# A hybrid encoder layer on one core: spectra from sums over even and odd samples, frequency pairs by sum and difference, and the inverse transform behind the second gate

## The chip, the cores and the metric

The kernel runs on one core of a Trainium2 chip. The metric is the time of one launch on the device in microseconds (us). TensorE (PE in the profile, PEld its weight loads) multiplies, VectorE (DVE) and ScalarE (ACT) do the elementwise work, SyncE (SP) issues nearly all loads. GpSimd does nothing here.

## The reference

One encoder layer over 256 tokens of width 1024, in float32: two mixers side by side, merged by gates, then 32 experts. The part that is changed is the long convolution of the Hyena mixer:

```python
z = (v * x1).astype(jnp.float32)
L = z.shape[1]
Z = jnp.fft.rfft(z, n=2 * L, axis=1)
K = jnp.fft.rfft(kern, n=2 * L, axis=0)
y = jnp.fft.irfft(Z * K[None], n=2 * L, axis=1)[:, :L] + z * hy_bias.astype(jnp.float32)
return y.astype(dt) * x0
...
o = o * jax.nn.silu(r)                                   # the other mixer (GLA), normalised
merged = jax.nn.sigmoid(g_gla) * (o_gla @ w_branch_gla) + jax.nn.sigmoid(g_hy) * (o_hy @ w_branch_hy)
h = h + merged @ w_out
h = h + moe_ffn(rms_norm(h, norm2_w), router_w, ...)     # top 4 of 32 experts
```

## The kernel before

Five programs, one per engine, walk the same list of stages (`schedule()`, `STAGES`) and do their share of each in that order; an engine never overtakes within its own list. Between engines stand semaphores.

The front (up to some 366 us) consists of projections with float32 precision made from three passes. Weights come in chunks of 1 MB (`FRONT`, `CHUNKS`) through four ring slots, so a chunk is loaded once the chunk four places ahead of it is used up. A chunk holds two units. For each unit ScalarE casts a high part (`parts`, L1266) and VectorE subtracts it for the low part (L1531); four such buffers exist (`HI_BUFS`), so the parts of a unit follow the use of the unit four places ahead. Units named `tok` take TensorE twelve matmuls of 512 columns. r 0 and r 1 (the silu gate of GLA) are eight such units, gg, wg, gh, wh (the two gates and the two branch matrices, each with halves 0 and 1) four units per half.

The Hyena convolution is a transform by matrix: the tokens are two blocks of 128 (`a`), the 256 odd frequencies of a 512-point transform two blocks of 128 (`kc`), with real and imaginary part (`ri`), the channels two halves of 512. `zt` transposes the product z to token-major tiles. `spectrum` (L791) gives one tile of K (the filter's) or Z (the signal's) from two accumulating matmuls, one per block of tokens. ScalarE copies the K tiles to SBUF; VectorE multiplies Z tiles in PSUM by them (L1694 to L1700, complex product). `zbias` scales z by the bias. The inverse (`y`, L975) is eight tiles of four matmuls, from which VectorE makes the Hyena outputs (L1708, L1711).

`gated` (L1671) multiplies the normalised GLA output by silu(r); `oT` transposes it on TensorE (L729) and waits for all eight operations of `gated` (`onorm_ready`). Before the change the stages run: zt, K, zbias, Z, r 0, r 1, gated, y, oT, gg 0, wg 0, gh 0, wh 0, gg 1, wg 1, gh 1, wh 1, wo (with the transposes mT of the merged tokens), router, experts.

In SP's list the loads of the front stop before chunk gh 0 for a wait on the Hyena outputs, since expert chunks go into ring slots that held the spectra:

```python
first_late = CHUNK_OF["gh0", 0]
for c in range(FSLOTS, first_late):
    front(c)

sp.wait_ge(ohy_ready, DB)
...
for c in range(first_late, len(CHUNKS)):
    for n in early[:1]:
        moe(n)
    early = early[1:]
    front(c)
```

`early` holds eight expert chunks of 1 MB. The other loads of the experts each wait until TensorE has used up what their slot held (`chunks_used`).

Of the kernel before, what the change touches and what calls it, by code (L numbers as in the profile page):

```python
# [97 lines left out]
def shape_tables():  # L98
# [11 lines left out]
    t[:, T_NEGT:T_NEGT + TB] = -lin.reshape(TB, P).T  # L110
# [4 lines left out]
    fwd = np.concatenate([np.cos(ang), np.sin(ang)], 1)  # L115
    inv = fwd.T / SEQ
    dft = np.concatenate([fwd.reshape(TB, P, 2 * SEQ).transpose(1, 0, 2).reshape(P, -1),
                          inv.reshape(4, P, SEQ).transpose(1, 0, 2).reshape(P, -1)], 1).astype(np.float32)
# [3 lines left out]
    z = np.concatenate([lin[:, None], np.cos(a), -np.sin(a)], 1).T.astype(np.float32)  # L122
    return np.ascontiguousarray(t), np.ascontiguousarray(dft), np.ascontiguousarray(z)
# [57 lines left out]
def schedule():  # L181
# [25 lines left out]
    for half in range(2):  # L207
        for k in ("gg", "wg", "gh", "wh"):
            if (k, half) == ("wh", 1):
                st += [("mT", 0), ("mT", 1)]  # L210
            st += tok(k, half)
            if (k, half) == ("wg", 0):
                st += [("ohy_parts",), ("bias_parts",)]
# [38 lines left out]
def tiles_of(stage):  # L252
# [8 lines left out]
    if kind in ("decay", "softplus", "energy", "energy_rest", "onorm", "gated", "zbias", "parts", "ohy_parts", "bias_parts", "wo"):  # L261
        return []
    if kind == "scores":
        return [f"sc{at[0]}", f"ke{at[0]}"]
    if kind == "updates":
        return [f"U{at[0]}{k}" for k in range(4)]
    if kind == "Z":
        return [f"Z{at[0]}{at[1]}{ri}" for ri in range(2)]
# [15 lines left out]
def build(nc, ins, out):  # L284
    plan, bank_uses = psum_plan()
    with ExitStack() as ctx:
# [62 lines left out]
        dft = hyreg(12288, 1024).rearrange("p (a k) -> p a k", a=TB)  # L349
        idft = hyreg(13312, 1024).rearrange("p (a t) -> p a t", a=4)  # L350
# [18 lines left out]
        ytmp = sumreg.rearrange("p (q a n) -> p q a n", q=2, a=2)  # L369
# [119 lines left out]
        z_ready = sem("z_ready")  # L489
        x0_ready = sem("x0_ready")  # L490
# [53 lines left out]
        def bank(name):  # L544
            return banks[plan[name][0]]
# [71 lines left out]
        def _(sp):  # L617
# [52 lines left out]
            sp.dma_start(hyreg(12288, 2048), ins["dft_table"]).then_inc(dft_loaded, 16)  # L670
# [48 lines left out]
        def _(pe):  # L719
# [114 lines left out]
            for stage in STAGES:  # L834
# [115 lines left out]
                elif kind == "zt":  # L950
# [3 lines left out]
                                                 zT[:, 4 * half + k, a * P:(a + 1) * P], ident) for k in range(4)])  # L954
                elif kind == "K":
                    ri, kc, half = at
                    pe.wait_ge(dft_loaded, 16)
                    pe.wait_ge(sd_ready, 2 * TB)
                    spectrum(f"K{ri}{kc}{half}", ri, kc,
                             lambda a: sumh[:, a, half * 512:(half + 1) * 512] if ri == 0 else  # L960
                             hf[:, a, D + half * 512:D + (half + 1) * 512])
                elif kind == "Z":
                    kc, half = at
                    if stage == ("Z", 0, 0):
                        for hh in range(2):
                            for a in range(TB):
                                emptied(pe, f"zt{a}{hh}")
# [956 lines left out]
```

## Time and profile before

| | |
|---|---|
| median of 3 runs | 1302.2 us (1301.52 to 1303.13) |
| the profiled execution | 1301.57 us, its span 1299.7 us |
| TensorE busy | 1201.0 us, 92% of the span |
| VectorE busy | 398.8 us, 31% |
| ScalarE busy | 264.7 us, 20% |
| moved from HBM | 454.26 MB, 350 GB/s over the span |
| TensorE's granted clock | 0.99 of full, mean of the span |

Busy time is the share in which an engine works on something; in which stretch it is the limit can't be told from it, only from the stretches and the chain of waits.

### The profile page before, as it was taken

Reading aid. Unit: us, or ns where it says so; the run is one execution under the profiler, and the core shown is the slowest. Engines: PE = TensorE matmul, PEld = TensorE weight load, DVE = VectorE, ACT = ScalarE, POOL = GpSimd, SP = SyncE. Lnnn points to the kernel's source line nnn. Section 1 sums busy time; section 2 is a strip of 40 time slices with the busy share of each in tenths; the row PEclk is TensorE's granted clock in tenths of the full one; section 3 lists DMA queues with packets and bytes.
Section 4 is the critical chain, followed back from the end, with each engine's and each line's share of the span. In section 5 each row is a group of like instructions: output and inputs, shape, how many; then the busy total and the mean of one; then the engine's idle time right before and its main releaser. Section 6 shows DMA issues by size and latency. Waiting matters only on the chain.

```text
span 1299.7 us, 14020 instructions
## 1 busy us (share of the span) xinstructions
PE 1201.0 (92%) x5992; PEld 619.0 (48%) x5992; DVE 398.8 (31%) x683; ACT 264.7 (20%) x398; POOL 0.2 (0%) x4
## 2 busy tenths in 40 slices
PE   6999999999999999999999888998898898889985
PEld 5889966888853343343334333332432243243321
DVE  6588837655541111121111111111111112111111
ACT  5855443344420010010001001000100010010001
POOL 0000000000000000000000000000000000000000
PEclk9999999999999989999999999999999999999999
DMA  9353423596599999999999999999999999999994
GB/s 328 106 153 109 143 76 98 176 385 209 198 352 407 425 410 428 428 429 427 429 427 428 427 428 428 429 427 427 429 427 428 427 427 428 427 428 429 428 426 202
DMA packets 66075, 456.25 MB, mean 351 GB/s; under 512 B 6777, under 2 KB 23450, under 8 KB 38876
## 3 DMA queue, kind: packets, MB, share of 16 engines
q1 hardware_dynamic: 64292, 454.52, 85.8%
q8 instruction: 49, 0.80, 0.3%
q10 hardware_dynamic: 1720, 0.82, 0.2%
q14 instruction: 14, 0.11, 0.0%
HBM read 454.26 MB, written 1.05 MB: 350 GB/s over the span
## 4 chain that ended last, share of the span: by engine, by line
PE 61%; DMA 29%; DVE 5%; ACT 3%; issue 2%; SPq 0%; ACTq 0%; DVEq 0%
DMA ring<-in_w_gate_up 28%; PE bank L1051 20%; PE bank L1067 12%; PE total L764 7%; PE bank L764 3%; PE total L752 3%; PE bank L752 3%; PE bank L807 3%; PE bank L1032 1%; PE bank L831 1%; PE bank L1058 1%; PE total L795 1%; PE bank L795 1%; ACT xn_area L1427 1%; PE total L1078 1%
## 5 line engine op out<-in xcount | busy, mean ns | idle before, releaser
L1051 PE MATMUL bank<-ring,hy_area 128*64 128x512 f32 x2048 | 456.9, 596 | 39.4 <-DMA ring<-in_w_gate_up 39.1
L1051 PEld LDWEIGHTS bank<-ring,hy_area 128*64 128x64 f32 x2048 | 140.1, 137 | 328.8 <-issue 248.1
L1067 PE MATMUL bank<-ring,xn_area 128*64 128x512 f32 x1024 | 231.5, 605 | 21.6 <-ACT xn_area L1427 21.6
L1830 DVE TENSOR_SCALAR qk_area<-bank 128x512 f32<-128x512 f32 x32 | 22.1, 692 | 426.4 <-PE bank L1051 426.4
L1067 PEld LDWEIGHTS bank<-ring,xn_area 128*64 128x64 f32 x1024 | 71.8, 139 | 159.9 <-issue 131.6
L1423 ACT ACTIVATE qk_area<-qk_area 128x512 f32<-128x512 f32 x32 | 20.2, 631 | 496.4 <-DVE qk_area L1830 496.4
L1843 DVE SCALAR_TENSOR_TENSOR xn_area_r<-bank,tmp_area,xn_area_r 128x512 fp32r<-128x512 f32 x32 | 24.0, 751 | 308.3 <-ACT xn_area_r L1432 308.3
L1531 DVE TENSOR_TENSOR front_r<-ring,slot_r 128x1024 fp32r<-128x1024 f32 x66 | 80.6, 1223 | 51.5 <-ACT slot_r L1266 51.5
L1266 ACT CAST slot_r<-ring 128x1024 fp32r<-128x1024 f32 x66 | 69.1, 1047 | 68.2 <-PE total L764 44.2
L1432 ACT ACTIVATE xn_area_r<-bank,tmp_area 128x512 fp32r<-128x512 f32 x32 | 22.0, 687 | 234.7 <-PE bank L1067 234.7
L831 PE MATMUL bank<-tmp_area_r 128*128 128x512 f32 x128 | 39.6, 432 | 7.0 <-DVE qk_area L1831 5.3
L764 PE MATMUL total<-front_r,slot_r 128*128 128x512 f32 x112 | 43.8, 391 | 0.0
L1078 PE MATMUL total<-xn_area_r 64*128 64x512 f32 x256 | 38.3, 417 | 1.7 <-DVE xn_area_r L1843 1.7
L1427 ACT COPY xn_area<-bank 128x512 f32<-128x512 f32 x32 | 18.8, 586 | 87.7 <-PE bank L1058 87.7
L1078 PEld LDWEIGHTS total<-xn_area_r 64*128 64x128 f32 x256 | 21.6, 184 | 30.5 <-issue 25.2
L764 PE MATMUL total<-slot_r 128*128 128x512 f32 x88 | 34.3, 390 | 0.0
L831 PEld LDWEIGHTS bank<-tmp_area_r 128*128 128x128 f32 x128 | 22.0, 192 | 21.6 <-DVE qk_area L1831 16.2
L1058 PE MATMUL bank<-tab,qk_area 128*128 128x128 f32 x128 | 23.4, 309 | 8.7 <-DVE qk_area L1838 8.7
L764 PE MATMUL total<-slot_r,xn_area_r 128*128 128x512 f32 x76 | 30.5, 402 | 1.0 <-DVE xn_area_r L1547 1.0
L1531 DVE TENSOR_TENSOR front_r<-ring,w_hi_late 128x1024 fp32r<-128x1024 f32 x22 | 26.9, 1223 | 14.6 <-ACT w_hi_late L1266 14.5
L764 PE MATMUL bank<-front_r,slot_r 128*128 128x512 f32 x80 | 31.3, 392 | 0.0
L1058 PEld LDWEIGHTS bank<-tab,qk_area 128*128 128x128 f32 x128 | 19.4, 209 | 18.9 <-issue 18.2
(323 smaller groups left out, 1208.0 us busy)
## 6 DMA issues: line engine op xcount, KB each, us to landing
ring<-in_w_gate_up SPq DMA_DIRECT2D x116, 2048.0 KB, 30.6
ring<-in_w_down SPq DMA_DIRECT2D x58, 2048.0 KB, 34.5
ring<-in_w_in SPq DMA_DIRECT2D x31, 1024.0 KB, 5.7
ring<-in_w_gate_up SPq DMA_DIRECT2D x24, 1024.0 KB, 8.9
ring<-in_w_down SPq DMA_DIRECT2D x12, 1024.0 KB, 8.1
ring<-in_w_branch_gla SPq DMA_DIRECT2D x4, 1024.0 KB, 7.2
ring<-in_w_branch_hy SPq DMA_DIRECT2D x4, 1024.0 KB, 5.9
ring<-in_w_out SPq DMA_DIRECT2D x4, 1024.0 KB, 5.2
```

What stands on the lines that cost most here:

```text
L752: last = pe.matmul(t[:, 0:SEQ], w[:, d, :], act[:, d, :], start=(m == 0 and d == 0), stop=(m == 2 and d == DB - 1))
L764: last = pe.matmul(bank(f"{kind}{half}{a}")[:, :], act[:, d, a * P:(a + 1) * P], w[:, i, :], start=(u == 0 and i == 0 and m == 0), stop=(u ...
L795: last = pe.matmul(t[:, :], dft[:, a, ri * SEQ + kc * P:ri * SEQ + (kc + 1) * P], src(a), start=(a == 0), stop=(a == TB - 1))
L807: last = pe.matmul(banks[bank_of][:, i * width:(i + 1) * width], src[:, a, d_cols(d)], moving, start=(m == 0 and a == 0), stop=(m == 1 and ...
L831: pe.matmul(banks[bk][:, :], b_pick[e % 2][:, bk * P:(bk + 1) * P], part, start=(m == 0), stop=(m == 1))
L1051: last = pe.matmul(banks[bk][half * CAP:(half + 1) * CAP, :], xeT[:, j, q, :], slot(where(j))[:, c:c + 512], start=False, stop=(j == GU_CH ...
L1058: last = pe.transpose(banks[3][:, c * P:(c + 1) * P], act[:, c:4 * P:4], ident)
L1067: last = pe.matmul(banks[2][half * CAP:(half + 1) * CAP, :], half_of(actT, f), slot(where(j))[:, c * D + half * 512:c * D + (half + 1) * 512],
L1078: last = pe.matmul(banks[4 + 2 * a + half], selT[r, q, a * P:(a + 1) * P], part[r, :], start=False, stop=True, skip_group_check=True)
L1266: nc.scalar.copy(unit_hi(j), unit_of(j)).then_inc(w_hi_ready, 1)
L1427: nc.scalar.copy(actT.rearrange("p c s -> p (c s)"), banks[3][:, :]).then_inc(actT_ready, 1)
L1531: nc.vector.tensor_tensor(unit_of(j, as_r["front"]), unit_of(j), unit_hi(j).bitcast(F32), ALU.subtract).then_inc(w_parts_ready, 1)
```

## The change

The block of tokens `a` is now a sample parity: token 2p + a in partition p. A frequency k and its mirror 255 - k have the same sum over even samples and the opposite one over odd samples (with the roles of sum and difference exchanged in the imaginary part). So one matmul per parity and part gives a tile `even` and a tile `odd`; their sum is the spectrum at the lower 128 frequencies, their difference that at the upper ones. ScalarE copies the odd tile to SBUF, VectorE adds and subtracts (`combine`). Z is then in SBUF (`zparts`), and its product with K (`Zmul`) is six operations of 2 x 512 columns per half of the channels. The stages now run: zt, K, Z, r 0 (first two units), Zmul 0, r 0 (rest), zbias, r 1 (first two units), Zmul 1, r 1 (rest), gated, oT, gg 0, wg 0, gg 1, y, wg 1, gh 0, wh 0, gh 1, wh 1, and the chunks of weights are loaded in this order. The tables, the filter features and the transposes are permuted to match.

```diff
-         ("gg0", "w_in", GG0), ("wg0", "w_branch_gla", 0), ("gh0", "w_in", GH0), ("wh0", "w_branch_hy", 0),
-         ("gg1", "w_in", GG0 + HALF), ("wg1", "w_branch_gla", HALF), ("gh1", "w_in", GH0 + HALF),
-         ("wh1", "w_branch_hy", HALF)]
+         ("gg0", "w_in", GG0), ("wg0", "w_branch_gla", 0), ("gg1", "w_in", GG0 + HALF), ("wg1", "w_branch_gla", HALF),
+         ("gh0", "w_in", GH0), ("wh0", "w_branch_hy", 0), ("gh1", "w_in", GH0 + HALF), ("wh1", "w_branch_hy", HALF)]
...
-    st += [("K", ri, kc, half) for ri in range(2) for kc in range(2) for half in range(2)] + [("zbias",)]
-    st += [("Z", kc, half) for kc in range(2) for half in range(2)]
-    st += tok("r", 0) + tok("r", 1) + [("gated",)]
-    st += [("y", b) for b in range(DB)] + [("oT", n) for n in range(4)]
...
+    st += [("K", ri, half) for ri in range(2) for half in range(2)] + [("Z", half) for half in range(2)]
+    r0, r1 = tok("r", 0), tok("r", 1)
+    st += r0[:2] + [("Zmul", 0)] + r0[2:] + [("zbias",)] + r1[:2] + [("Zmul", 1)] + r1[2:] + [("gated",)]
+    st += [("oT", n) for n in range(4)] + tok("gg", 0) + tok("wg", 0) + tok("gg", 1)
+    st += [("y", b) for b in range(DB)] + tok("wg", 1) + [("ohy_parts",)] + tok("gh", 0) + [("bias_parts",)] + tok("wh", 0)
+    st += tok("gh", 1) + [("mT", 0), ("mT", 1)] + tok("wh", 1)
...
-            sp.dma_start(hyreg(12288, 2048), ins["dft_table"]).then_inc(dft_loaded, 16)
+            sp.dma_start(hyreg(12288, 1536), ins["dft_table"]).then_inc(dft_loaded, 16)
...
-            def spectrum(name, ri, kc, src):
-
-                t = begin(name)
-                for a in range(TB):
-                    last = pe.matmul(t[:, :], dft[:, a, ri * SEQ + kc * P:ri * SEQ + (kc + 1) * P], src(a),
-                                     start=(a == 0), stop=(a == TB - 1))
-                last.then_inc(fill(name), 1)
+            def spectrum(name, ri, a, src):
+
+                pe.matmul(begin(name)[:, :], dft[:, a, ri * P:(ri + 1) * P], src, start=True, stop=True).then_inc(fill(name), 1)
...
-                                                 zT[:, 4 * half + k, a * P:(a + 1) * P], ident) for k in range(4)])
+                                                 zT[:, 4 * half + k, a::TB], ident) for k in range(4)])
...
-                    pe.wait_ge(Y_ready, 4)
+                    pe.wait_ge(Y_ready, b // 4 + 1)
...
+            def combine(even, odd, ri, plus, minus):
+
+                filled(dve, even)
+                emptied(dve, odd)
+                nc.vector.tensor_tensor(plus, bank(even)[:, :], minus, ALU.add)
+                if ri == 0:
+                    last = nc.vector.tensor_tensor(minus, bank(even)[:, :], minus, ALU.subtract)
+                else:
+                    last = nc.vector.tensor_tensor(minus, minus, bank(even)[:, :], ALU.subtract)
+                last.then_inc(empty(even), 1)
...
+                elif kind == "Zmul":
+                    half, = at
                     cs = slice(half * 512, (half + 1) * 512)
...
+                    emptied(dve, "K110")
+                    emptied(dve, f"Z{half}10")
+                    zr, zi = zparts[half][:, 0], zparts[half][:, 1]
+                    kr, ki = Kf[:, 0, :, cs], Kf[:, 1, :, cs]
+                    nc.vector.tensor_tensor(Yf[:, 0, :, cs], zr, kr, ALU.mult)
+                    link(nc.vector.tensor_tensor(Yf[:, 1, :, cs], zr, ki, ALU.mult))
+                    nc.vector.tensor_tensor(zr, zi, ki, ALU.mult)
+                    nc.vector.tensor_tensor(zi, zi, kr, ALU.mult).then_inc(z_multiplied, 1)
+                    dve.wait_ge(z_multiplied, half + 1)
+                    nc.vector.tensor_tensor(Yf[:, 0, :, cs], Yf[:, 0, :, cs], zr, ALU.subtract)
+                    nc.vector.tensor_tensor(Yf[:, 1, :, cs], Yf[:, 1, :, cs], zi, ALU.add).then_inc(Y_ready, 1)
```

The instructions move as the following listings of the two programs show (in order, without times). First VectorE from the end of the spectra to `gated` in the kernel before. L1531 is the low part of a unit, L1731 the product of r with its sigmoid, L1671 `gated`.

```order
L1699 TENSOR_TENSOR ring<-ring 128x512
L1700 TENSOR_TENSOR ring<-ring 128x512
L1531 TENSOR_TENSOR front_r<-ring,slot_r 128x1024 x3
L1731 TENSOR_TENSOR gla_area<-total,tmp_area 128x512 x2
L1531 TENSOR_TENSOR front_r<-ring,w_hi_late 128x1024
L1531 TENSOR_TENSOR front_r<-ring,slot_r 128x1024 x3
L1731 TENSOR_TENSOR gla_area<-total,tmp_area 128x512 x2
L1531 TENSOR_TENSOR front_r<-ring,w_hi_late 128x1024
L1671 SCALAR_TENSOR_TENSOR v_area<-v_area,small,gla_area 128x256 x8
L1708 SCALAR_TENSOR_TENSOR ring<-bank,small,ring 128x256
L1711 TENSOR_TENSOR hy_area<-ring,hy_area 128x256
```

In the changed kernel the same place begins with the parts of two units and the six operations of Zmul 0. L1542 is the low part of a unit, L1746 the product of r, L1690 `zbias`.

```order
L1542 TENSOR_TENSOR front_r<-ring,slot_r 128x1024 x2
L1708 TENSOR_TENSOR ring<-gla_area,ring 128x2x512
L1709 TENSOR_TENSOR ring<-gla_area,ring 128x2x512
L1710 TENSOR_TENSOR gla_area<-gla_area,ring 128x1024
L1711 TENSOR_TENSOR gla_area<-gla_area,ring 128x1024
L1713 TENSOR_TENSOR ring<-ring,gla_area 128x2x512
L1714 TENSOR_TENSOR ring<-ring,gla_area 128x2x512
L1542 TENSOR_TENSOR front_r<-ring,slot_r 128x1024
L1746 TENSOR_TENSOR gla_area<-total,tmp_area 128x512 x2
L1542 TENSOR_TENSOR front_r<-ring,w_hi_late 128x1024
L1690 TENSOR_SCALAR ring<-ring,colw 128x256 x8
```

The list goes on with two parts and the first five operations of Zmul 1; from its sixth on it reads as follows, with L1682 as `gated` and L1558 as the first work behind `oT`.

```order
L1714 TENSOR_TENSOR ring<-ring 128x2x512
L1542 TENSOR_TENSOR front_r<-ring,slot_r 128x1024
L1746 TENSOR_TENSOR gla_area<-total,tmp_area 128x512 x2
L1542 TENSOR_TENSOR front_r<-ring,w_hi_late 128x1024
L1682 SCALAR_TENSOR_TENSOR v_area<-v_area,small,gla_area 128x256 x8
L1558 SCALAR_TENSOR_TENSOR gla_area_r<-bank,colw,v_area_r 128x256 x8
```

The two blocks of six now stand between the parts, and `gated` comes behind both of them; before, nothing of the spectra stood behind the first part of these.

SP's queue around the wait for the Hyena outputs, before: the wait stands ahead of the first row with `in_b_gate_up`, L654 is an expert chunk, L635 a front chunk.

```order
L635 DMA ring<-in_w_branch_gla 128x4x512 x2
L677 DMA tmp_area<-in_b_gate_up 128x512
L654 DMA ring<-in_w_gate_up 128x2048
L635 DMA ring<-in_w_in 128x4x512
L654 DMA ring<-in_w_gate_up 128x2048
L635 DMA ring<-in_w_in 128x4x512
```

And in the changed kernel:

```order
L635 DMA ring<-in_w_in 128x4x512 x2
L635 DMA ring<-in_w_branch_gla 128x4x512 x2
L677 DMA tmp_area<-in_b_gate_up 128x512
L654 DMA ring<-in_w_gate_up 128x2048
L635 DMA ring<-in_w_in 128x4x512
L654 DMA ring<-in_w_gate_up 128x2048
L635 DMA ring<-in_w_in 128x4x512
```

The chunks of gg 1 and wg 1 have moved ahead of the wait; the chunks behind it begin with gh 0 as before. Between the inverse and gh 0 TensorE had eight units (gg 0, wg 0); now it has four (wg 1).

## Rows read from the trace of the kernel before

**Rows 1.** first line of the page

```profile
span 1299.7 us, 14020 instructions
```

**Rows 2.** stretches: us, busy (instructions) of PE, PEld, DVE, ACT, POOL, granted clock, DMA share, GB/s

```profile
178.00:206.00 28.00, 28.00 (x72) 12.70 (x70) 12.48 (x28) 7.13 (x15) 0.00 (x0) 1.00 0.07 26
...
228.00:242.00 14.00, 14.00 (x67) 12.29 (x66) 11.36 (x26) 1.53 (x2) 0.00 (x0) 1.00 0.22 75
266.00:288.00 22.00, 22.00 (x98) 18.04 (x97) 11.91 (x11) 11.66 (x13) 0.00 (x0) 1.00 1.02 381
...
700.00:1250.00 550.00, 492.70 (x2315) 186.76 (x2311) 87.21 (x159) 42.07 (x72) 0.00 (x0) 0.99 1.01 428
```

**Rows 3.** chain of waits, 170 to 400 us: start us, us, what

```profile
178.70 6.87 PE total L795 x16
...
206.16 21.98 PE total L764 x96
228.14 6.91 PE bank L975 x32
...
241.95 1.75 PE bank L729 x16
...
367.80 1.94 PE bank L1051 x8
```

**Rows 4.** order of time, VectorE, 168 to 262 us: start us, busy us, line, operation

```profile
178.84 2.19 DVE L1679 TENSOR_SCALAR ring<-ring,colw 128x256 f32<-128x256 f32 x8
196.00 0.69 DVE L1694 TENSOR_TENSOR ring<-total,ring 128x512 f32<-128x512 f32 x1 [14.97 <-PE total L795]
196.61 0.68 DVE L1695 TENSOR_TENSOR ring<-total,ring 128x512 f32<-128x512 f32 x1
...
197.81 0.68 DVE L1697 TENSOR_TENSOR ring<-total,ring 128x512 f32<-128x512 f32 x1
198.52 0.69 DVE L1699 TENSOR_TENSOR ring<-ring 128x512 f32<-128x512 f32 x1
...
212.80 1.23 DVE L1531 TENSOR_TENSOR front_r<-ring,slot_r 128x1024 fp32r<-128x1024 f32 x1 [0.68 <-ACT slot_r L1266]
...
230.94 3.25 DVE L1671 SCALAR_TENSOR_TENSOR v_area<-v_area,small,gla_area 128x256 f32<-128x256 f32 x8
234.11 0.48 DVE L1708 SCALAR_TENSOR_TENSOR ring<-bank,small,ring 128x256 f32<-128x256 f32 x1
```

**Rows 5.** order of time, VectorE, 66 to 84 us

```profile
78.59 1.22 DVE L1597 TENSOR_TENSOR gla_area<-gla_area 128x1024 f32<-128x1024 f32 x1
79.72 1.22 DVE L1597 TENSOR_TENSOR ring<-ring 128x1024 f32<-128x1024 f32 x1
```

**Rows 6.** chain of waits, 78 to 104 us

```profile
85.56 7.45 PE bank L752 x48
...
97.18 5.75 PE total L752 x48
```

**Rows 7.** order of time, TensorE, 78 to 100 us (in brackets: idle before)

```profile
85.56 2.01 PE L752 MATMUL bank<-xn_area_r,slot_r 128*128 128x256 f32 x8 [1.97 <-DVE tmp_area L1639]
```

**Rows 8.** stretches, columns as in the second group

```profile
86.00:88.00 2.00, 2.00 (x11) 2.00 (x10) 1.97 (x4) 0.00 (x0) 0.00 (x0) 0.50 0.57 200
```

**Rows 9.** order of time, SP's queue, 0 to 480 us: issues

```profile
243.35 0.43 SPq L654 DMA_DIRECT2D ring<-in_w_gate_up  x1
...
276.71 0.38 SPq L635 DMA_DIRECT2D ring<-in_w_in  x1
```

**Rows 10.** order of time, ScalarE, 262 to 290 us

```profile
286.80 1.05 ACT L1266 CAST slot_r<-ring 128x1024 fp32r<-128x1024 f32 x1 [3.49 <-DMA ring<-in_w_in]
```

**Rows 11.** the line that loads front chunks (L635)

```profile
DMA to landing us min/median/max: 5.0/5.7/12.2
```

**Rows 12.** DMA issues, 240 to 300 us: queue, size of one, us to landing

```profile
tmp_area<-in_norm_f_w ACTq DMA_DIRECT2D x1, 512.0 KB, 17.3
...
tmp_area<-in_router_w ACTq DMA_DIRECT2D x1, 128.0 KB, 8.2
```

More of the change, by code:

```diff
@@ L114, in shape_tables @@
     ang = np.arange(SEQ)[:, None] * w[None, :]
[L115 to L118, printed above, removed]
+    fwd = np.concatenate([np.cos(ang[:, 0:P]), np.sin(ang[:, 0:P])], 1)
+    inv = (np.concatenate([np.cos(ang), np.sin(ang)], 1).T / SEQ).reshape(2, 2, P, SEQ)
+    inv[:, 1] = inv[:, 1, ::-1].copy()
+    dft = np.concatenate([fwd.reshape(P, 2 * SEQ), inv.reshape(4, P, SEQ).transpose(1, 0, 2).reshape(P, -1)], 1).astype(np.float32)
     omega = (np.float32(2.0 * np.pi) * np.arange(SEQ, dtype=np.float32) / np.float32(SEQ)).astype(np.float32)
@@ L122, in shape_tables @@
     z = np.concatenate([lin[:, None], np.cos(a), -np.sin(a)], 1).T.astype(np.float32)
+    z = np.concatenate([z[:, k::TB] for k in range(TB)], 1)
     return np.ascontiguousarray(t), np.ascontiguousarray(dft), np.ascontiguousarray(z)
@@ L260, in tiles_of @@
         return []
-    if kind in ("decay", "softplus", "energy", "energy_rest", "onorm", "gated", "zbias", "parts", "ohy_parts", "bias_parts", "wo"):
+    if kind in ("decay", "softplus", "energy", "energy_rest", "onorm", "gated", "zbias", "Zmul", "parts", "ohy_parts", "bias_parts", "wo"):
         return []
@@ L266, in tiles_of @@
         return [f"U{at[0]}{k}" for k in range(4)]
+    if kind == "K":
+        return [f"K{at[0]}{at[1]}{a}" for a in range(TB)]
     if kind == "Z":
-        return [f"Z{at[0]}{at[1]}{ri}" for ri in range(2)]
+        return [f"Z{at[0]}{ri}{a}" for ri in range(2) for a in range(TB)]
     return [kind + "".join(map(str, at))]
@@ L368, in build @@
         xbuf = ring[:, 4 * SLOT + 1024:5 * SLOT].rearrange("p (b t) -> p b t", b=4)
-        ytmp = sumreg.rearrange("p (q a n) -> p q a n", q=2, a=2)
+        zparts = [m.rearrange("p (r k n) -> p r k n", r=2, k=2) for m in (gla_area[:, :], sumreg)]
         zfeat = tmp_area[0:EMB, 0:SEQ]
@@ L489, in build @@
         z_ready = sem("z_ready")
+        z_multiplied = sem("z_multiplied")
         x0_ready = sem("x0_ready")
@@ L1333, in _ @@
                 elif kind == "K":
-                    ri, kc, half = at
-                    n = f"K{ri}{kc}{half}"
-                    copy_tile(n, Kf[:, ri, kc, half * 512:(half + 1) * 512], bank(n)[:, :])
+                    ri, half = at
+                    n = f"K{ri}{half}1"
+                    copy_tile(n, Kf[:, ri, 1, half * 512:(half + 1) * 512], bank(n)[:, :])
+                elif kind == "Z":
+                    half, = at
+                    for ri in range(2):
+                        n = f"Z{half}{ri}1"
+                        copy_tile(n, zparts[half][:, ri, 1, :], bank(n)[:, :])
                 elif kind == "zt":
@@ L1404, in _ @@
                         elif nm == "gg":
-                            emptied(sc, f"wh0{a}" if half else f"r1{a}")
+                            emptied(sc, f"wg0{a}" if half else f"r1{a}")
                             sigmoid_tile(n, a, empty(n))
                         elif nm == "gh":
-                            emptied(sc, f"wg{half}{a}")
+                            emptied(sc, f"wh0{a}" if half else f"wg1{a}")
                             sigmoid_tile(n, a, empty(n))
@@ new lines, in _ @@
+                elif kind == "K":
+                    ri, half = at
+                    even, odd = f"K{ri}{half}0", f"K{ri}{half}1"
+                    plus, minus = (Kf[:, ri, k, half * 512:(half + 1) * 512] for k in range(2))
+                    combine(even, odd, ri, plus, minus)
+                elif kind == "Z":
+                    half, = at
+                    for ri in range(2):
+                        combine(f"Z{half}{ri}0", f"Z{half}{ri}1", ri, zparts[half][:, ri, 0, :], zparts[half][:, ri, 1, :])
+                elif kind == "Zmul":
+                    half, = at
+                    cs = slice(half * 512, (half + 1) * 512)
+                    emptied(dve, "K110")
[9 more added lines that the diff above has]
+                    nc.vector.tensor_tensor(Yf[:, 1, :, cs], Yf[:, 1, :, cs], zi, ALU.add).then_inc(Y_ready, 1)
```

50 lines of the change are left out of this document (12 added, 38 removed).

## The prediction

> **What bounds the kernel now.** First the stretches, for who is busy where [rows 2]. In the spectra (178 to 206 us) and the inverse (228 to 242) TensorE is busy all of the time at the full clock while the DMA engines are nearly idle (share 0.07 and 0.22); from 266 to 288 TensorE is full and so are the DMA engines, at 381 GB/s; from 700 us on the DMA engines are full at 428 GB/s and TensorE has holes. So two bounds follow each other: TensorE up to the experts, the expert weights behind it. Then the chain of waits, for what links the pieces [rows 3]: spectra, r units, inverse, oT, gates follow one another on TensorE with no wait between. The expert stream can't start before that chain is through, because the expert chunks reuse ring slots which the queue frees by TensorE's progress. Its length is bytes over 428 GB/s. I therefore take a shift of TensorE's chain ahead of the experts one to one into the end. The profiled execution took 1301.57 us with a span of 1299.7 us [rows 1]; the median of the three runs is 0.6 us higher.
>
> **What is removed.** The spectra, four pieces of the chain like the first (6.87 us), from 178.70 us to the start of r at 206.16 us, are 32 matmuls of 512 columns: 27.5 us, 0.86 us each [rows 3]. The change issues 16. TensorE saves 13.7 us and would start r at 192.4 us. Each even/odd pair takes TensorE 1.72 us, ScalarE one copy, VectorE two operations that start 0.60 us apart [rows 4]: 1.2 us per pair, so VectorE keeps up here, and it ends the eighth pair near 194 us.
>
> **What is added, and where it lies.** The product of spectra was 24 operations of 512 columns on VectorE, most of it under the second half of the spectra. Now it is two blocks (Zmul) of six operations of 1024 columns, each block in VectorE's queue ahead of work that TensorE needs. Prices: 512 columns, starts 0.60 us apart, 0.71 us where a semaphore is waited for; a 1024 column operation from SBUF to SBUF, starts 1.13 us apart [rows 4, 5]. A block is 6 x 1.13 plus two waits of 0.11: 7.0 us.
>
> VectorE before Zmul 0 must do the parts of two r1 units. In the trace the second of these starts 6.64 us after r begins (212.80 against 206.16) [rows 3, 4] and waits for ScalarE, not for VectorE's queue. So it starts at 192.4 + 6.6 = 199.1, and Zmul 0 at 200.2. From there VectorE never waits; the queue in order of the listing is
>
> 7.0 (Zmul 0) + 1.1 (part) + 1.2 (two r products) + 1.1 (part) + 2.3 (zbias, 2.19 and its wait [rows 4]) + 2.3 (two parts) + 7.0 (Zmul 1) + 1.1 + 1.2 + 1.1 + 3.2 (gated, 230.94 to 234.11 [rows 4]) = 28.7 us,
>
> so gated ends at 228.9 us. The r units on TensorE take 21.98 us and end at 214.4. Their weights come just in time: the third r1 unit's part is done at 207.2 + 1.2 = 208.4, TensorE asks for it after six units of 2.75 us at 208.9. Behind r the next thing on TensorE is oT, which waits for all of gated, and in its queue stand gg 0 and everything else. Before, the inverse transform (228.14 to 241.95, 13.8 us [rows 3]) lay over gated and hid it; the change has moved that cover behind gg 1. TensorE idles from 214.4 to 229.0: 14.6 us. oT began at 241.95 with the inverse done; it now begins at 229.0 with 13.8 us of inverse owed: 242.8. **First term: +0.9 us**, the saved 13.7 us are gone in this wait.
>
> On these durations the Trainium skill (VectorE: DVE Perf Modes, The DRAIN you can't avoid) says that the next operation can't start before the pipe of the last one is empty, so that starts would stand a whole duration apart. The rows show 0.60 us between starts of operations that last 0.69 us, so the measurement decides; by the page the 28.7 us would be about 31 and the total some 2.4 us later.
>
> **The clock after the wait.** The one place ahead of the experts where TensorE, after steady work, stood still for about 2 us is at 83.6: restarted at 85.56, it was granted 0.50 of its clock (1.2 GHz) and 48 matmuls took 7.45 us, the same 48 later 5.75 us [rows 6 to 8]. That is 1.7 us for a wait of 2.0 us; a wait of 14.6 us should cost as much. No row shows a wait that long, so the bounds are 0 and, if the transposes of oT (1.75 us) also run at half speed beside it, 3.5 us. **Second term: +1.7 us.**
>
> **The weights behind the inverse.** SP waits for the last of the hyena outputs before it issues the bias, the first expert chunk and then chunk gh 0. It is a wait that stands ahead of all later loads. Before, it ended at 243.35, 1.4 us after the inverse, and gh 0 was 22 us away. Now the inverse ends with only wg 1 (11.0 us) ahead of gh 0. Call the inverse's end 0. First expert chunk issued at 1.4; a 1 MB load alone lands in 5.0 us [rows 9, 11]; chunk gh 0 lies behind it, 1.05 MB at 381 GB/s, 2.75 us: 9.2. Cast and part 2.3 us: ready at 11.5, wanted at 11.0. Stall 0.5 us. After that each chunk comes with an expert chunk, 2.1 MB at 381 GB/s, 5.5 us, exactly what TensorE needs for two units. Before, a chunk issued at 276.71 was waited for by ScalarE until 286.80, ten microseconds [rows 9, 10], and TensorE lost nothing since its lead was larger. Now that lead is gone, and the router's and norm's loads (128 and 512 KB from ScalarE's queue, the latter 17.3 us in flight [rows 12]) fall in the middle: 1.7 us at that rate, of which I count 1.5. **Third term: +2.0 us**; bounds 0 (the stream catches up, as 428 GB/s would allow) and 4 (the inefficient small loads cost double).
>
> The Trainium skill (DMA: Bandwidth & Descriptors, Specifications) names a limit of about 358 GB/s of HBM per core; by it a pair would take 5.9 us, and eight pairs would add some 3 us more. The trace has 381 to 428 GB/s on one core, above that limit, and I don't use it.
>
> **Edits at nothing.** The transform table is 0.25 MB shorter: it was loaded 160 us before its use. Strided transposes (zt): the same four tiles; TensorE's price of a step of two isn't in the trace, below 1.8 us if it doubled and 0 if it is free; I take 0, since the combination of halves is what follows. The swap of gg 1/wg 1 with gh 0/wh 0 keeps the number of units. zbias is counted above. The inverse's own products on VectorE stay hidden under its matmuls, as now. ScalarE's cast of the hyena outputs (and VectorE's part of it) now stands behind the gh 0 casts and so behind their loads; it is wanted at wh 0, 11 us after gh 0 begins, and stays hidden unless that chunk is several microseconds late.
>
> **Sum.** 1301.6 + 0.9 + 1.7 + 2.0 = 1306.2 us for the profiled execution, so 1306.5 us beside the median.
>
> **Rivals.**
> - *VectorE keeps up, faster.* If the queue from 200.2 were done by 214.4, the whole 13.7 us would be kept, less the third term: 1302.2 - 11.7 = 1290.5 us. For it the 28.7 us of work would have to be 14.2. To come out faster by over 2.6 us it must be under 21.5 us. Single steps are measured, and even the twelve operations of 1024 columns at half their price (as zbias, one-source, runs 256 columns in 0.27 us) give back only 6.4 us. The Trainium skill (VectorE: DVE Perf Modes, The perf-mode tier table) gives that double rate in fp32 to one-source operations and not to tensor_tensor. Chance 0.07.
> - *No change.* The first term alone, with the clock quickly back and the loads hidden: 1303.1 us; up to 1304.8 with one of them. For it speaks that both other terms are small against their uncertainty. Chance 0.20.
> - *Much slower.* The stalls in gh and wh are long enough to bring the half clock once more for each (1.7 us), and the small loads cost double: 1306.5 + 2 + 1.7 = 1310 us or more. Against it: the waits are under 1 us each. Chance 0.10.
> - *Forecast.* 1304.8 to 1309.5 us. Chance 0.60. The remaining 0.03 is for faster by a part of the queue, around 1298 us.
>
> **How the numbers follow.** This kernel's three runs lie about 0.1% apart, so a difference of 0.2% (2.6 us) can be told. Faster 0.10, same 0.20, slower 0.70. For 8 in 10 the range takes in the forecast, the no-change case and the near part of much slower: 1302.6 to 1310.0 us.
>
> **What will show it.** (1) Spectra: 16 matmuls, r starting near 192.4. (2) Zmul operations starting 1.13 us apart, VectorE without a gap from 200 to 229. (3) TensorE waiting some 14 us at oT for VectorE's gated. If that wait is under 7 us, the forecast is wrong. (4) granted clock 0.5 behind it. (5) a wait for DMA on the way to gh 0, and later ones of a microsecond at most. (6) the experts' first matmul, at 367.80 before [rows 3], near 372.4. If TensorE's chain is late by that but the end isn't, the one-to-one step is wrong.

## The result and the profile after

The changed kernel takes 1310.85 us (median of 8 runs, 1306.93 to 1312.68) against 1302.25 us before (8 runs, 1301.52 to 1305.97): 1.0058 times as long, 95% interval [1.0042, 1.0073]. It is slower, by 0.6%. The median lies 0.85 us above the top of the range (1310.0), and in the rival *much slower* (1310 us or more) rather than in the forecast (1304.8 to 1309.5); the ratio times the 1302.2 us that the prediction stood against is 1309.8, just inside the range. The profiled execution took 1308.84 us, 7.3 us more than the profiled one of before and inside the forecast.

First the chain of waits of the changed kernel, 170 to 400 us (start us, us, what). L793 are the spectra, L764 the units, L729 the transposes, L970 the inverse.

```profile
176.76 2.01 PE bank L729 x16
178.76 3.44 PE total L793 x8
...
192.50 5.50 PE total L764 x24
...
225.85 3.26 DVE v_area L1682 x8
229.16 3.68 PE bank L729 x16
232.83 22.14 PE total L764 x96
...
265.97 3.45 PE bank L970 x16
...
279.78 11.01 PE bank L764 x48
290.79 2.15 issue
292.94 23.86 PE total L764 x96
...
374.93 1.94 PE bank L1046 x8
```

Against [rows 3]: the spectra take 13.7 us, not 27.5, and r starts at 192.50 instead of 206.16. But the chain then leaves TensorE: from 200 us on it runs through VectorE up to `gated`, and oT (L729) starts at 229.16. The same 16 transposes that took 1.75 us now take 3.68. A piece called "issue" (time in which the engine waited for nothing that the profile shows) stands ahead of gh 0, and the 96 matmuls behind it take 23.86 us where their like take 21.99. The experts' first matmul stands at 374.93 against 367.80, 7.13 us later.

TensorE's waits of the changed kernel (us in total, times, longest) name the two new ones; the first is for `gated`.

```profile
PE bank L729 <- DVE v_area L1682: 14.6, 1, 14.6
...
PE total L764 <- issue: 2.2, 1, 2.2
```

VectorE of the changed kernel in order of time, 200 to 232 us:

```profile
200.30 1.22 DVE L1708 TENSOR_TENSOR ring<-gla_area,ring 128x1024 f32<-128x1024 f32 x1
201.43 1.22 DVE L1709 TENSOR_TENSOR ring<-gla_area,ring 128x1024 f32<-128x1024 f32 x1
...
210.82 2.19 DVE L1690 TENSOR_SCALAR ring<-ring,colw 128x256 f32<-128x256 f32 x8
213.05 2.36 DVE L1542 TENSOR_TENSOR front_r<-ring,slot_r 128x1024 fp32r<-128x1024 f32 x2
215.32 1.22 DVE L1708 TENSOR_TENSOR ring<-ring 128x1024 f32<-128x1024 f32 x1
...
225.85 3.25 DVE L1682 SCALAR_TENSOR_TENSOR v_area<-v_area,small,gla_area 128x256 f32<-128x256 f32 x8
```

From the row at 200.30 on no row ends in a bracket, and a bracket would name idle time: VectorE is occupied from Zmul 0 (L1708, 200.30) to the end of `gated` (229.1), 28.8 us without a gap. That answers to the queue that was summed from [rows 4, 5].

The stretches of the changed kernel (columns as in [rows 2]):

```profile
214.00:229.00 15.00, 0.51 (x3) 0.08 (x1) 14.93 (x20) 1.53 (x2) 0.00 (x0) 0.68 0.22 70
229.00:232.00 3.00, 2.84 (x14) 2.85 (x15) 0.10 (x1) 0.00 (x0) 0.00 (x0) 0.50 0.00 0
289.00:312.00 23.00, 20.85 (x84) 16.65 (x83) 13.45 (x12) 12.05 (x13) 0.00 (x0) 0.93 1.03 405
...
700.00:1250.00 550.00, 495.35 (x2324) 190.06 (x2325) 86.71 (x160) 42.24 (x72) 0.00 (x0) 0.98 1.01 428
```

The first row is the swap of bounds in one line: TensorE 0.51 us busy, VectorE 14.93 of 15. The second is the clock behind it, 0.50 (1.2 GHz). The last shows the experts as before, 428 GB/s: from the experts' first matmul to the end of the span it is 932.1 us (1307.0 - 374.93), before 931.9.

Last the loads behind the inverse: SP's queue of the changed kernel in order of time, ScalarE's first cast of gh 0, and the time from issue to landing (last number, us) of the first expert chunk and of the first chunk of gh 0. They answer to [rows 9 to 12].

```profile
280.79 0.34 SPq L677 DMA_DIRECT2D tmp_area<-in_b_gate_up  x1
281.18 0.43 SPq L654 DMA_DIRECT2D ring<-in_w_gate_up  x1
281.65 0.43 SPq L635 DMA_DIRECT2D ring<-in_w_in  x1
282.13 0.50 SPq L654 DMA_DIRECT2D ring<-in_w_gate_up  x1
```

```profile
290.54 1.99 ACT L1261 CAST slot_r<-ring 128x1024 fp32r<-128x1024 f32 x2 [22.95 <-DMA ring<-in_w_in]
```

```profile
ring<-in_w_gate_up SPq DMA_DIRECT2D x1, 1024.0 KB, 6.7
ring<-in_w_in SPq DMA_DIRECT2D x1, 1024.0 KB, 8.9
```

The first chunk of gh 0 is issued at 281.65 and in use at 290.54, as soon as it has landed: 8.9 us. TensorE asked for its parts at 290.79 and got them at 292.94.

### The profile page after: what moved, and what is told of

The parts are those of the page before. It is cut to its first block, busy times and chain, and to the rows that moved or that the text cites. A ratio compares the mean times of both kernels' runs of the same rounds, so it can differ in the third digit from the quotient of the medians.

```text
span 1307.0 us, 13963 instructions
## 1 busy us (share of the span) xinstructions
PE 1193.2 (91%) x5960; PEld 616.9 (47%) x5960; DVE 407.3 (31%) x687; ACT 263.8 (20%) x398; POOL 0.2 (0%) x4
## 4 chain that ended last, share of the span: by engine, by line
PE 59%; DMA 29%; DVE 7%; ACT 3%; issue 2%; SPq 0%; DVEq 0%; ACTq 0%
DMA ring<-in_w_gate_up 28%; PE bank L1046 20%; PE bank L1062 12%; PE total L764 6%; PE bank L764 3%; PE total L752 3%; PE bank L752 3%; PE bank L803 3%; PE bank L1027 1%; PE bank L827 1%; PE bank L1053 1%; DVE front_r L1542 1%; ACT xn_area L1427 1%; PE total L1073 1%; DMA ring<-in_w_in 1%
## 5 line engine op out<-in xcount | busy, mean ns | idle before, releaser
L1062 PE MATMUL bank<-ring,xn_area 128*64 128x512 f32 x1024 | 234.2, 611 | 21.6 <-ACT xn_area L1427 21.6
L1542 DVE TENSOR_TENSOR front_r<-ring,slot_r 128x1024 fp32r<-128x1024 f32 x66 | 80.2, 1222 | 58.2 <-ACT slot_r L1261 58.1
L764 PE MATMUL total<-front_r,slot_r 128*128 128x512 f32 x128 | 50.8, 396 | 0.0
L764 PE MATMUL total<-slot_r 128*128 128x512 f32 x100 | 39.6, 396 | 0.0
L764 PE MATMUL total<-slot_r,xn_area_r 128*128 128x512 f32 x76 | 31.5, 415 | 3.1 <-issue 2.2
L1542 DVE TENSOR_TENSOR front_r<-ring,w_hi_late 128x1024 fp32r<-128x1024 f32 x22 | 26.9, 1222 | 12.3 <-ACT w_hi_late L1261 12.3
L764 PEld LDWEIGHTS total<-front_r,slot_r 128*128 128x128 f32 x128 | 24.6, 192 | 5.3 <-issue 0.2
## 6 DMA issues: line engine op xcount, KB each, us to landing
ring<-in_w_branch_hy SPq DMA_DIRECT2D x4, 1024.0 KB, 13.8
```

Of the source, the lines that this page charges most:

```text
L764: last = pe.matmul(bank(f"{kind}{half}{a}")[:, :], act[:, d, a * P:(a + 1) * P], w[:, i, :], start=(u == 0 and i == 0 and m == 0), stop=(u ...
L1062: last = pe.matmul(banks[2][half * CAP:(half + 1) * CAP, :], half_of(actT, f), slot(where(j))[:, c * D + half * 512:c * D + (half + 1) * 512],
L1542: nc.vector.tensor_tensor(unit_of(j, as_r["front"]), unit_of(j), unit_hi(j).bitcast(F32), ALU.subtract).then_inc(w_parts_ready, 1)
```

## The experiments

The theory on trial is that of the prediction: VectorE's queue up to `gated` bounds TensorE, the clock falls in the wait, and chunk gh 0 is late. The rivals: the order of the stages costs the time whatever VectorE does; the even and odd spectra cost it; the loads alone do. Each kernel below is timed beside the kernel before on the same chip.

**Zmul 1 behind `gated`.** It takes six operations of 1024 columns out of the queue ahead of `gated`.

```diff
-    st += r0[:2] + [("Zmul", 0)] + r0[2:] + [("zbias",)] + r1[:2] + [("Zmul", 1)] + r1[2:] + [("gated",)]
+    st += r0[:2] + [("Zmul", 0)] + r0[2:] + [("zbias",)] + r1 + [("gated",), ("Zmul", 1)]
```

> The changed kernel with Zmul 1 moved behind gated in the list of stages, nothing else. Theory (VectorE's queue from Zmul 0 to gated is the wait at oT): the queue is 7.0 us shorter, oT is released near 222.1 us instead of 229.1, TensorE's wait there falls from 14.6 to 7.6 us, the half clock behind it stays, and the whole is 7 us shorter than the changed kernel: about 1304 us beside its median of 1311, ratio to the kernel before 1.001. Rival (oT is held by something other than that queue, such as r's last product or the banks): the wait stays near 14.6 us and the time near 1311 us, ratio 1.006.

Measured: 1301.77 us (11 runs) beside 1302.53 (19 runs), ratio 0.9994 [0.9983, 1.0005]. The median is 2.2 us below the 1304 us expected. TensorE's wait at oT and the chain of waits:

```profile
PE bank L729 <- DVE v_area L1682: 7.6, 1, 7.6
```

```profile
221.89 3.68 PE bank L729 x16
...
283.82 2.18 issue
286.00 22.20 PE total L764 x96
```

The wait fell by 7.0 us, the price of one block, and oT starts 7.3 us sooner. So VectorE's queue is what TensorE waits for there, and one block is enough to bring back the time of before. Half the wait costs the same half clock (3.68 us again). The rest of the gain, to 8.5 us at the experts' first matmul (366.40), is that the 2.18 us at gh 0 brought no half clock this time: 22.20 us instead of 23.86. Some 0.3 us of it was lost again in gg 0 and wg 0 (22.44 us instead of 22.14).

**The chunks of gh 0 ahead of SP's wait.** Both chunks of gh 0 are issued before SP waits for the Hyena outputs.

```diff
-            first_late = CHUNK_OF["gh0", 0]
+            first_late = CHUNK_OF["wh0", 0]
```

> The changed kernel, but SP issues the two chunks of gh 0 before its wait for the Hyena outputs. Theory (the wait ahead of these loads costs a stall and a half clock): the stall of 2.15 us ahead of gh 0 and the 1.9 us of half clock behind it go, 4 us less than the changed kernel: 1307 us, ratio 1.003. Rival (the DMA engines are too slow for front and expert chunks together): the stall appears at wh 0 or gh 1 instead, with its half clock, and the time stays at 1311, ratio 1.006.

Measured: 1306.38 us (9 runs) beside the same 1302.53, ratio 1.0029 [1.0019, 1.0038]. The chain of waits has no piece ahead of gh 0 any more, and its units are at their full rate:

```profile
278.81 11.01 PE bank L764 x48
289.81 21.99 PE total L764 x96
```

From the end of wg 1 to the first matmul of the experts it is 80.1 us (289.82 to 369.92), in the changed kernel 84.1 (290.79 to 374.93): in the traces the late chunk costs 4.0 us, 2.15 of wait and 1.87 of half clock. The medians bear out the direction and not the size: this one is 4.5 us below the changed kernel's first median and 1.7 below the one of the second series (1308.12, below). The wait at oT stays at 14.7 us; the two are independent of each other.

**The order alone.** The spectra of before (four accumulating pairs and a VectorE product under them) in the changed order: oT, gg 0, wg 0, gg 1, y, wg 1, gh 0, with the chunks and ScalarE's waits to match.

```diff
-    st += [("y", b) for b in range(DB)] + [("oT", n) for n in range(4)]
...
+    st += [("oT", n) for n in range(4)] + tok("gg", 0) + tok("wg", 0) + tok("gg", 1)
+    st += [("y", b) for b in range(DB)] + tok("wg", 1) + [("ohy_parts",)] + tok("gh", 0) + [("bias_parts",)] + tok("wh", 0)
```

> The kernel before with only the order changed: the inverse behind gg 1, gg 1 and wg 1 ahead of gh 0, the loads in that order; spectra and products as before. Theory: r ends at 228.1, gated at 234.1, so TensorE waits 6.0 us at oT, which the inverse covered; half clock 2.0 us; gh 0 late and half clock 4.0 us: 12 us slower than before, about 1314 us, ratio 1.009. Rival (the order is harmless and the spectra's form costs the time): within 3 us of the kernel before, ratio 1.000 to 1.002.

Measured: 1312.54 us (5 runs) beside 1302.53, ratio 1.0079 [1.0064, 1.0093]. Chain of waits:

```profile
230.78 3.26 DVE v_area L1665 x8
...
234.08 3.30 PE bank L723 x16
...
295.17 0.79 issue
```

Here `gated` (L1665) ends where it ended before, and oT (L723) stands directly behind it: TensorE waits 6.1 us, with r ended at 228.0. Before, those 6.1 us lay under the inverse. With the inverse owed, oT comes 5.9 us later than before (234.08 + 13.81 against 241.95), its transposes take 1.55 us more, and most of the rest are two waits of 0.8 us for parts of gh 0 and behind. So the order by itself costs 10 us; 12 were expected, since the wait at gh 0 was taken over from the changed kernel. SP issues the same loads here in the same rhythm (first expert chunk at 285.56, chunk gh 0 at 286.03), but they land sooner, measured from issue as above:

```profile
ring<-in_w_gate_up SPq DMA_DIRECT2D x1, 1024.0 KB, 5.3
ring<-in_w_in SPq DMA_DIRECT2D x1, 1024.0 KB, 7.5
```

**The spectra alone.** The changed kernel with the order of before: y ahead of oT, then gg 0, wg 0, gh 0, wh 0 and the second halves. All of the even and odd work and both Zmul blocks stay where the change put them.

```diff
-    st += [("oT", n) for n in range(4)] + tok("gg", 0) + tok("wg", 0) + tok("gg", 1)
-    st += [("y", b) for b in range(DB)] + tok("wg", 1) + [("ohy_parts",)] + tok("gh", 0) + [("bias_parts",)] + tok("wh", 0)
...
+    st += [("y", b) for b in range(DB)] + [("oT", n) for n in range(4)]
```

> The changed kernel with the order undone: the inverse directly behind r and gated, gates and loads in the order of before; spectra from even and odd samples, sums and differences and the Zmul blocks stay. Theory: TensorE does the inverse's first half from 214.4, waits about 1 us for Zmul 1 (222.4), ends the inverse near 229.3; oT follows gated and the inverse's first products on VectorE, done near 232.6; gg 0 starts near 233.1 instead of 243.7, and gh 0 has its lead again: 10.6 us less than before, about 1291.7 us, ratio 0.992. Rival (the Zmul blocks on VectorE cost what the halved spectra save): ratio 0.999 to 1.003.

Measured: 1290.86 us (5 runs) beside 1302.53, ratio 0.9909 [0.9896, 0.9923]. TensorE in order of time (L976 is the inverse, L735 oT; in brackets the idle time before):

```profile
222.24 7.17 PE L976 MATMUL total<-ring 128*128 128x256 f32 x32 [1.12 <-DVE ring L1720]
230.22 0.63 PE L735 MATMUL bank<-tab,v_area 128*128 128x128 f32 x4 [0.23 <-DVE ring L1728]
```

The inverse stands over `gated` again, and what is left of the wait is 1.1 us for Zmul 1 in the middle of the inverse and under 1 us around oT. gg 0 starts at 232.78, the first matmul of the experts at 357.12, 10.7 us earlier than before. This is 20.0 us faster than the changed kernel's first median and 17.3 us faster than its second, from the order alone. The rival in which VectorE keeps up was worked out to 1290.5 us. That the measured time is so near is in part chance: its sum has the third term (2.0 us), which this kernel doesn't pay, and of the 13.7 us saved it loses 3.0 up to the experts, 2.0 of them in these waits.

**The changed kernel once more, and the wait filled.** The first of these is the kernel unaltered, to have its time beside the next ones. The second puts 16 matmuls of 512 columns, whose results are overwritten, ahead of oT's wait. TensorE then has something to do in it; nothing on VectorE moves.

```diff
+                    if stage == ("oT", 0):
+                        t = begin("oT0")
+                        for _ in range(16):
+                            pe.matmul(t[:, :], ident, tab[:, 0:512], start=True, stop=True)
                     pe.wait_ge(onorm_ready, 8)
```

> The changed kernel once more, unaltered, for a second trace. Its eight runs fall into two groups (1307 to 1309 and 1310 to 1313 us). In the traces so far the stretch from the experts' first matmul to the end took 931.9 to 932.1 us, but 936.7 in one run in which TensorE was at 0.91 of its clock in the first 80 us of it. If the spread lies there, a run near 1311 us has about 935 us in this stretch and the front up to 375 us as before; if it lies ahead of it (the terms of the prediction vary), the experts begin near 378 us.

> The changed kernel, with 16 more matmuls (identity times a table, 13.7 us, into the bank that oT overwrites) on TensorE ahead of its wait at oT; they add nothing to the result. Theory of the clock: the wait of TensorE shrinks to 0.9 us, oT takes 1.75 instead of 3.68 us, gg 0 starts 2.1 us earlier: 1308.8 us. Rival (oT is slow for another reason, its operands or its banks): oT stays at 3.7 us.

Measured: unaltered 1308.12 us (10 runs), ratio 1.0045 [1.003, 1.006] to 1302.6 (21 runs); filled 1309.55 us (6 runs), ratio 1.0045 [1.0028, 1.0063]. Stretches of the filled one:

```profile
214.00:228.00 14.00, 13.31 (x32) 5.54 (x30) 13.93 (x19) 1.20 (x2) 0.00 (x0) 1.00 0.22 75
228.00:231.00 3.00, 2.79 (x21) 2.62 (x22) 0.15 (x1) 0.79 (x3) 0.00 (x0) 1.00 0.00 0
...
390.00:397.00 7.00, 6.31 (x20) 2.37 (x20) 1.87 (x4) 0.59 (x1) 0.00 (x0) 0.56 0.77 324
```

Chain of waits:

```profile
228.21 1.97 PE bank L729 x16
...
287.98 1.31 issue
289.30 22.24 PE total L764 x96
```

With TensorE busy up to 0.9 us before `gated` ends, oT runs at the full clock and takes 1.97 us instead of 3.68: the idling is what took the clock, and the term is 1.7 us in oT and some 0.1 in the 96 matmuls behind it (22.00 us, 22.14 and 22.05 unfilled). At the experts' first matmul (370.39) the kernel is 4.0 us ahead of the unaltered one (374.43). Only 1.8 us of that are this term: the wait at gh 0 was also shorter (1.31 us, 2.26 in the unaltered kernel), with 0.25 us of half clock behind it and not 1.83, and another wait of 0.5 us came ahead of wh 1. The time at the end doesn't show the gain: 1308.8 us were expected, from the first median of 1310.85, and beside the second the filled kernel isn't faster at all. From there to the end of the span it takes 937.2 us, not 931.8. The third row above is where it begins: 20 us into the experts TensorE is at 0.56 of its clock, the DMA share falls to 0.77, and in the first 50 us of the experts 375 GB/s are moved where the changed kernel moves 388 and the kernel before 393. I had not foreseen that, and come back to it below.

**zbias ahead of the spectra, in the spectra alone.** The eight operations of `zbias` go in front of K, where VectorE has time.

```diff
-    st += [("K", ri, half) for ri in range(2) for half in range(2)] + [("Z", half) for half in range(2)]
+    st += [("zbias",)] + [("K", ri, half) for ri in range(2) for half in range(2)] + [("Z", half) for half in range(2)]
...
-    st += r0[:2] + [("Zmul", 0)] + r0[2:] + [("zbias",)] + r1[:2] + [("Zmul", 1)] + r1[2:] + [("gated",)]
+    st += r0[:2] + [("Zmul", 0)] + r0[2:] + r1[:2] + [("Zmul", 1)] + r1[2:] + [("gated",)]
```

> The spectra alone (order of before), with zbias put back ahead of the spectra, where VectorE stands idle for 2.6 us. Theory of the queue: Zmul 1 is done at 220.1, before TensorE asks for it (221.3), gated ends near 226.8, gg 0 starts near 230.9 instead of 232.8: 1289.0 us, 1.9 us less than without, ratio 0.9895. Rival (what is left there is TensorE's own work): 1290.9, ratio 0.991.

Measured: 1292.24 us (6 runs, 1288.87 to 1293.88) beside 1302.6, ratio 0.9916 [0.9897, 0.9936]. Its profiled execution took 1288.87 us (1289.0 expected), gg 0 started at 230.98, 1.8 us ahead of 232.78, and the wait for Zmul 1 was gone, which is what moving 2.2 us of VectorE out of the queue should give. The median doesn't confirm a gain: the six times lie in two groups, 1288.9 to 1290.9 and 1293.6 to 1293.9. Between this kernel and the spectra alone the runs don't decide.

**The changed order, mended.** Zmul 1 behind `gated`, zbias ahead of K, chunks of gh 0 ahead of SP's wait: all three edits above, in the changed kernel.

> The changed order with all three remedies: Zmul 1 behind gated, zbias ahead of the spectra, the two chunks of gh 0 ahead of SP's wait. The queue up to gated is 28.7 - 7.0 - 2.3 = 19.4 us, the wait at oT falls to 5.3 us, the half clock behind it stays, nothing waits at gh 0: 14.6 - 5.3 + 4.0 = 13.3 us less than the changed kernel, about 1297 us, ratio 0.996. Rival (the terms hide one another): not under 1300 us.

Measured: 1296.47 us (6 runs) beside 1302.6, ratio 0.9948 [0.9931, 0.9965]. Chain of waits:

```profile
216.85 3.26 DVE v_area L1682 x8
220.15 3.67 PE bank L729 x16
223.83 22.40 PE total L764 x96
...
282.04 21.99 PE total L764 x96
```

About 1297 us were expected. The change can be made to pay with its own order, but 5.6 us (medians) less than the spectra alone, and 4.2 less than those with `zbias` early, which were timed in the same series. Of the wait at oT 6.1 us remain (5.3 expected), the same as with the order alone: it is the length of the last products of r, a part and `gated` behind the end of r, which no place for Zmul shortens, and it costs the half clock in oT (3.67 us) once more. That part belongs to a unit behind oT; `gated` ahead of it in VectorE's list wasn't tried.

## Why the prediction was right, and where it wasn't

The table has every profiled kernel at the three places that count, in us: start of oT, first matmul of the experts, and from there to the end of the span.

| kernel | oT | experts | to the end | its run | median |
|---|---|---|---|---|---|
| before | 241.95 | 367.80 | 931.9 | 1301.57 | 1302.25 |
| changed | 229.16 | 374.93 | 932.1 | 1308.84 | 1310.85 |
| changed again | 228.68 | 374.43 | 931.8 | 1308.05 | 1308.12 |
| Zmul 1 behind gated | 221.89 | 366.40 | 936.7 | 1304.87 | 1301.77 |
| gh 0 chunks ahead | 228.72 | 369.92 | 932.0 | 1303.79 | 1306.38 |
| order alone | 234.08 | 377.71 | 933.0 | 1312.54 | 1312.54 |
| spectra alone | y first | 357.12 | 931.9 | 1290.86 | 1290.86 |
| zbias early | y first | 355.28 | 931.8 | 1288.87 | 1292.24 |
| order mended | 220.15 | 362.18 | 932.5 | 1296.53 | 1296.47 |
| wait filled | 228.21 | 370.39 | 937.2 | 1309.54 | 1309.55 |

*What is removed*: right. 13.7 us of matmuls are gone, r starts at 192.50 (192.4 said).

*VectorE's queue*: right in its parts and its sum. Zmul operations start 1.13 to 1.26 us apart; the queue took 28.8 us (28.7 said; its parts as they are printed add up to 28.6) and TensorE waited 14.6 us (14.6 said). The **first term** was +0.9 and measured +1.0: 229.16 + 13.81 of inverse owed, less 241.95. That the wait is VectorE's is shown by taking one block out of the queue (7.0 us less wait), and that the inverse was the cover by giving it back (spectra alone). The Trainium skill (VectorE: DVE Perf Modes, The DRAIN you can't avoid) has the next operation start when the pipe of the one before is empty, but adds that one which isn't held back starts earlier. The prediction left the second half out. The trace agrees with it: 1.22 us operations start 1.13 us apart (200.30, 201.43), and 28.8 us stand against the estimate of 31 by the first half alone. One example in the rival *VectorE keeps up* was misread as well: 256 columns in 0.27 us is 1.1 us for 1024, the price of the operations in Zmul and not half of it.

*The clock after the wait*: right. The **second term** was +1.7 and measured +2.1: 1.93 in oT, 0.15 in gg 0. A wait of 14.6 us costs about what one of 2.0 us did in [rows 6] (1.7 us), as assumed. The filled wait shows that idling is the cause. That any wait of about 2 us does this isn't shown (see the last section).

*The weights behind the inverse*: the place and the mechanism were right, the size was not. This **third term** was mis-sized: +2.0 said, +4.0 measured, just at the bound of 4. It was made of 0.5 us of stall and 1.5 us for the router's and norm's loads. The runs showed the other way round. The stall was 2.15 us: with the inverse ended at 279.78, chunk gh 0 was in use 10.8 us later and not 9.2. The step behind that is the landing of the expert chunk ahead of it, 6.7 us where the 5.0 of a lone load was taken; chunk gh 0 followed it by 2.7 us, as said (2.75). The expert chunk took 6.7 to 6.8 us in three traces (changed, again, Zmul 1 behind `gated`), but 5.3 in the order alone and 5.6 in the filled kernel, behind the same bias and with the same chunks issued behind it; the stall was 0.79 and 1.31 us there. So neither the bias nor the four chunks issued within 1.5 us (281.18 to 282.68) explain the 6.7 us by themselves; why it differs stays open. And the stall brought 1.87 us of half clock, which was put into the rival *much slower*, on the reason that waits under 1 us bring none. The 1.5 us for the small loads never appeared: from the start of gg 0 to the experts' first matmul it was 124.1 us before (243.70 to 367.80); after it is 142.1 us, and less the inverse (13.81), the stall (2.15) and the two half clocks (1.87 and 0.15) that is 124.1 again. The chunks ahead of SP's wait gave this term back in the trace.

The Trainium skill (DMA: Bandwidth & Descriptors, Specifications) has about 358 GB/s of HBM as the limit for a core; the changed kernel's trace has 405 GB/s in 289 to 312 us and 428 in the experts on its one core, so the measurement decides against it as a limit here, and no stall past gh 0 came.

*One to one to the end*: right for the profiled executions, 932.1 against 931.9 us. 1.0 + 2.1 + 4.0 = 7.1 us is the whole of 374.93 - 367.80. It is not a law: the column "to the end" has two entries that are 5 us longer, and one that is 1.1 us longer.

*The sum*: the prediction says that the median was 0.6 us above the profiled execution, which makes 1306.8 us beside the median and not 1306.5; nothing hangs on it.

*Edits at nothing*: the strided transposes of z cost 0.2 us (2.01 for 16 against 1.80 before), bound 1.8; the others nothing that shows.

*The median*: 1310.85, 2.0 us above its own profiled execution, and 1308.12 when run again. The times of this kernel spread over nearly 6 us: 1306.9 to 1312.7 in the first series and 1306.6 to 1312.2 in the second, with a gap in the middle each time (1308.8 to 1310.3, 1309.3 to 1311.3); which side holds the median moves it. The kernel before spreads as much in the experiments' series, without such a gap (1300.6 to 1306.1, and one of 1308.2). Both traces of the changed kernel were from the lower side, so what its longer executions do wasn't seen. So the terms are tested on the profiled execution, 1306.2 said and 1308.84 measured, and not on whether the median falls inside the range.

Where did the gain go, then? The spectra alone are worth 11.7 us. The order alone costs 10.0. Together they should come out near 1301, and the unaltered kernel is 7 to 10 us above that (1308.12, 1310.85). The rest is the two meeting, in the traces 6.4 us up to the start of gg 0 and 1.6 at gh 0, where the order alone lost 2.4 us and the changed kernel 4.0. For the first: the spectra's work moved into VectorE's queue between r and `gated`, and the order took away the 13.8 us of TensorE's work that would have hidden it. Either alone can be afforded.

## What to carry to other kernels

Work taken off the busy engine and put on an idle one belongs behind the last thing that the busy engine will ask the idle one for, or under work that covers it, as in the spectra alone; the idle engine's average (31% here) says nothing about its queue in that stretch. Before a stage is moved, add up what it covered at its old place, on every engine and queue; here the inverse covered 6.1 us of the last step of the gate even before anything was added. Try the parts of a combined change one by one: half of this one is 0.9% faster, the other half 0.8% slower.

## What the runs showed of the hardware

**The same short wait has different prices.** At gh 0 TensorE waited 2.15 us in the changed kernel and 2.26 us when it was run again, and the next 96 matmuls took 23.86 and 23.82 us (the granted clock was 0.86 in 293 to 295 us and 0.50 in 295 to 297, so it fell after the restart, not in the wait). With Zmul 1 moved the wait was 2.18 us and the matmuls took 22.20, at a clock of 1.00 in 286 to 292. A 1.3 us wait in the filled kernel cost 0.25 us. The kernel before has such a pair too: the wait of 1.97 us of [rows 7] was followed by 0.50, one of 1.76 us that ended at 25.55 by a clock of 1.00 in 26 to 28. What decides between them isn't shown. At oT every unfilled wait, from 6.1 to 14.7 us, was followed by it (0.50 to 0.58 in the 3 us behind), and the transposes took 3.30 to 3.68 us instead of 1.75.

**Half clock at the start of the DMA-bound stage isn't given back.** The two long entries of the table both have it. Chain of waits and stretches of the kernel with Zmul 1 behind `gated`:

```profile
388.57 9.63 PE bank L1062 x32
```

```profile
383.00:390.00 7.00, 6.31 (x34) 3.72 (x30) 3.91 (x7) 1.21 (x2) 0.00 (x0) 0.78 1.01 425
390.00:397.00 7.00, 7.00 (x26) 2.07 (x24) 0.00 (x0) 0.00 (x0) 0.00 (x0) 0.73 0.78 286
```

TensorE is granted 0.73 to 0.78 and takes 9.63 us for the 32 matmuls that took 7.09 before. In 390 to 397 it is busy all of the time, so it isn't waiting for loads; it uses up its chunks more slowly, and since a chunk's slot must be empty before the next load starts, the DMA engines go short: a share of 0.78 and 286 GB/s, where the kernel before has this at the same distance from its first expert matmul:

```profile
392.00:399.00 7.00, 7.00 (x33) 2.25 (x31) 1.14 (x2) 0.69 (x1) 0.00 (x0) 1.00 0.95 330
```

In the first 50 us of the experts that is 378 GB/s against 393, 0.75 MB less. The shortfall grows to 1.3 MB by 160 us (405 GB/s on the mean of them against 413) and is never made up while the DMA engines are full: the last wait for an expert chunk ends 909.8 us behind the experts' first matmul (1276.19), 906.7 before (1274.52). That is 3.1 us. The rest stands behind the last load, in the last 32 matmuls of the same kind, first before and then with Zmul 1 moved:

```profile
1282.54 7.11 PE bank L1067 x32
```

```profile
1284.21 8.81 PE bank L1062 x32
```

They are at half the clock again in part (0.58 in 1284 to 1288 us, before 1.00 in 1282.5 to 1286.5) and take 1.7 us longer. 3.1 and 1.7 are the 4.8 us. In the filled kernel the same two are 3.8 and 1.5 us, the 5.3 of its column; the order alone and the order mended have the second only (8.56 and 8.81 us). What makes the clock fall in these places isn't shown.

Whether this goes with the kernel or with the single execution isn't shown. All six times of the filled kernel lie between 1308.9 and 1310.3, and none near the 1304 us that its front alone would give; the eleven of the kernel with Zmul 1 moved run from 1300.3 to 1305.4, with the profiled one (1304.87) near the top. That the spread of the times and this episode are the same thing is argued from two traces, not shown.
